# Reordered splits, stores and roundings at eleven places of a GLA + latent-attention inference step

## The reference

```
gla_mixer:  q, k, v, r = h @ w_q, h @ w_k, h @ w_v, h @ w_r
            lg = log_sigmoid((h @ w_gk1) @ w_gk2 + b_gk) / 16
            b = cumsum(lg) within a chunk of 64;  k*exp(-b), q*exp(b), k*exp(b_last-b)
            o, S = recurrence over the chunks;  out = (rmsnorm(o) * silu(r)) @ w_o
mla_mixer:  cq = rmsnorm(h @ w_dq);  q = cq @ w_uq;  q_rope = rope(q[..., 128:])
            q_abs = q_nope @ w_uk;  scores over 4096 cached rows (paged) + new rows
            out = softmax(scores) @ ckv @ w_uv @ w_o
conv_ffn:   u = h @ w_gate;  c = conv_b + causal taps of width 3 over u
            out = (gelu(c) * (h @ w_up)) @ w_down
trunk:      layer 0: x += norm(gla(norm x));  x += norm(conv_ffn(norm x))
            layer 1: x += norm(mla(norm x));  x += norm(conv_ffn(norm x))
```

## Time and profile before

| what | value |
|---|---|
| median of 3 runs | 1475.28 us (1474.13 to 1475.62) |
| the profiled execution's own time | 1475.53 us |
| its span on the core | 1473.8 us |
| TensorE, VectorE, ScalarE, GpSimd busy | 97%, 62%, 46%, 38% |
| mean granted TensorE clock | 0.995 |
| moved by DMA | 160.19 MB, 109 GB/s |

### The profile page before, as it was taken

How to read it: one execution, slowest core, us unless ns; L and a number is a source line. 1 busy time by engine, 2 the same in 40 slices (tenths; PEclk the granted TensorE clock), 3 DMA queues, 4 the chain that set the end, 5 groups by cost and what they waited for, 6 DMA issues and landing times. The chain is left out here.

```text
span 1473.8 us, 31036 instructions
## 1 busy us (share of the span) xinstructions
PE 1428.7 (97%) x11156; PEld 1304.1 (88%) x11156; DVE 916.4 (62%) x1506; ACT 676.6 (46%) x1281; POOL 561.1 (38%) x552
## 2 busy tenths in 40 slices
PE   6999999999999999999999999999999999999997
PEld 6999998988999999998986566666989999999997
DVE  4742446499999993236466744433579999995223
ACT  5433345375666672216313444443265565665211
POOL 1333111235555554341330044441315555554433
PEclk9999999999999999999999999999999999999999
DMA  4242322213232323222321099981212323223231
GB/s 165 72 144 86 115 86 101 91 58 104 97 103 96 103 88 112 97 79 96 104 81 33 4 283 287 280 261 46 102 47 87 115 85 114 85 84 109 82 98 66
DMA packets 56714, 160.19 MB, mean 109 GB/s; under 512 B 7633, under 2 KB 27602, under 8 KB 55330
## 3 DMA queue, kind: packets, MB, share of 16 engines
q1 hardware_dynamic: 50466, 137.82, 28.1%
q0 software_dynamic: 6144, 20.98, 4.6%
HBM read 150.72 MB, written 8.05 MB: 108 GB/s over the span
## 5 line engine op out<-in xcount | busy, mean ns | idle before, releaser
L716 POOL TENSOR_TENSOR w_l<-w_raw,w_h 128x1408 fp32r<-128x1408 f32 (+1 forms) x50 | 143.8, 2878 | 274.8 <-ACT w_h L837 153.3
L711 POOL TENSOR_TENSOR w_l<-w_raw,w_h 128x1024 fp32r<-128x1024 f32 (+2 forms) x42 | 108.1, 2575 | 284.1 <-ACT w_h L837 274.3
L2272 PE MATMUL lin<-xg_h,w_h 128*128 128x272 f32 x848 | 195.4, 303 | 17.1 <-DVE xg_l L1449 10.6
L2272 PE MATMUL lin<-xg_l,w_h 128*128 128x272 f32 x848 | 184.7, 290 | 0.0
L2272 PE MATMUL lin<-xg_h,w_l 128*128 128x272 f32 x848 | 184.6, 290 | 0.0
L2625 PE MATMUL lin<-xq_h,wq_r 128*128 128x272 f32 x864 | 170.1, 289 | 3.7 <-DVE xq_l L1835 3.6
L2625 PE MATMUL lin<-xq_h,w_h 128*128 128x272 f32 x576 | 166.3, 289 | 2.4 <-DVE xq_l L1835 2.3
L2625 PE MATMUL lin<-xq_h,w_l 128*128 128x272 f32 x576 | 166.0, 288 | 0.0
L2625 PE MATMUL lin<-xq_l,w_h 128*128 128x272 f32 x576 | 165.4, 287 | 0.0
L2272 PEld LDWEIGHTS lin<-xg_h,w_h 128*128 128x128 f32 x848 | 138.2, 191 | 25.0 <-issue 13.5
L837 ACT ACTIVATE w_h<-w_raw 128x1024 fp32r<-128x1024 f32 (+2 forms) x71 | 77.2, 1088 | 171.1 <-PE lin L2272 139.1
(11 more groups left out here) (407 smaller groups left out, 3238.4 us busy)
## 6 DMA issues: line engine op xcount, KB each, us to landing
wq_raw<-w SPq DMA_DIRECT2D x38, 1024.0 KB, 5.0
w_raw<-w SPq DMA_DIRECT2D x61, 512.0 KB, 3.5
w_raw<-w SPq DMA_DIRECT2D x30, 704.0 KB, 4.1
pages<-cache SPq DMA_DIRECT2D x128, 160.0 KB, 3.8
pages<-cache POOLq DMA_DIRECT2D x128, 160.0 KB, 3.8
St<-state SPq DMA_DIRECT2D x4, 1024.0 KB, 6.0
gla_s<-St SPq DMA_DIRECT2D x4, 1024.0 KB, 3.9
w_raw<-w SPq DMA_DIRECT2D x4, 576.0 KB, 3.8
```

Source lines behind the costliest of these rows:

```text
L711: g.tensor_tensor(w_l[:, p % 2, 0:n], raw_panel(p)[:, 0:n], w_h[:, p % 2, 0:n].bitcast(F32), ALU.subtract).then_inc(w_lo, 1)
L716: g.tensor_tensor(w_l[:, p % 2, 0:n], w_raw[:, p % 2, 0:n], w_h[:, p % 2, 0:n].bitcast(F32), ALU.subtract).then_inc(w_lo, 1)
L2272: last = mm(lin[:, 2 * out_set + half, 0:HALF], w[:, slot, (w0 + k) * P:(w0 + k + 1) * P], (v[ch] if isinstance(v, list) else v[:, ch, :]) ...
```

## The change

Nothing is computed differently; instructions of one engine change places, and a few waits move with them. The places, in order of the program: (A) ACT splits panel 1 after chunk 5 of x, not chunk 3, and TensorE sums the squares two steps later. (B) DVE makes the running sums of the gates of head 0 one step sooner. (C) SP loads panel `P_G2 + 3` ahead of the last state's store; ACT waits for the store's landing behind the split of panel `P_G2 + 2`, still ahead of the squares; DVE updates the last sample state ahead of `gated_lo(5)`, two groups of instructions sooner. (D) In the third direct product, the second tile's chunk 6 is multiplied after the first tile's last chunk. (E) In both layers, ACT and DVE make the first pair's quarters ahead of some work on plain channel 3. (F) Of the keys of each two heads, the first are copied out between the two products of a rotation. (G) At the end of the prompt's attention the order of the last `probs` and of the last heads' rounding changes. (H) `score_unit` takes its three waits one by one, each before the matmuls that need it. (I) At the last unit of pages ACT splits `P_M3` before `page_probs`, and TensorE's first half of that panel is cut in chunks 4, 2 and 2 instead of 5, 2 and 1.

```diff
--- before.py
+++ after.py
@@ -591,10 +591,11 @@
     load_panel(P_G2 + 2, io["w8"][P_G2 + 2])
+    load_panel(P_G2 + 3, io["w8"][P_G2 + 3])
     state_out(3)
...
     sp_.dma_start(io["gla_p"], S[:]).then_inc(gla_out, 16)
-    load_run(io["w8"], P_G2 + 3, P_G2 + 3, P_F0A - P_G2 - 4)
+    load_run(io["w8"], P_G2 + 4, P_G2 + 4, P_F0A - P_G2 - 5)
     for k in range(3):
@@ -945,7 +946,7 @@
             square(i, x[:, i, :])
-        if chs[0] == 2:
+        if chs[0] == 4:
             split_hi(1)
@@ -1064,11 +1065,12 @@
             split_hi(p0 + m + 2)
+            if n == 1 and m == 0:
+                act.wait_ge(st_out[0], 32)
             act.wait_ge(evac, t0 + m + 1)
...
-    act.wait_ge(st_out[0], 32)
     output_squares(P_G2, T_G2, 1, ("ffn_pre", 0))
@@ -1199,10 +1201,11 @@
         quarter_hi(None, 0, 0)
+        quarter_hi(None, 0, 1)
         plain_tap(3)
-        quarter_hi(None, 0, 1)
         quarter_hi(None, 0, 2)
         quarter_hi(None, 0, 3)
+        quarter_hi(None, 0, 4)
@@ -1222,13 +1225,12 @@
         part(None, 0, 0)
-        quarter_hi(None, 0, 4)
         quarter_hi(None, 0, 5)
         part(None, 0, 1)
-        plain_gelu(3)
         input_hi(5)
...
         quarter_hi(None, 0, 6)
+        plain_gelu(3)
         input_hi(6)
@@ -1344,12 +1346,18 @@
     probs(0)
-    for n in range(NM):
-        if n + 1 < NM:
-            probs(n + 1)
+    for n in range(NM - TILES):
+        probs(n + 1)
         if n % TILES == 1 and n > TILES:
...
         probs_turned(n)
+    probs(NM - 3)
+    probs(NM - 2)
+    probs_turned(NM - 4)
+    probs(NM - 1)
+    for n in range(NM - 3, NM):
+        probs_turned(n)
+    head_hi(H_M - 2)
     head_hi(H_M - 1)
@@ -1393,9 +1401,10 @@
         pages_turned(4 * unit_ + 3)
+    act.wait_ge(qk_ps, UNITS)
+    split_hi(P_M3)
     page_probs(UNITS - 1)
     page_probs_turned(UNITS - 1)
-    split_hi(P_M3)
     split_hi(P_M3 + 1)
@@ -1546,8 +1555,8 @@
             gate((t - 1) // 2)
-        if t in (2, 4, 6, 8):
-            gate_sums((t - 2) // 2)
+        if t in (1, 4, 6, 8):
+            gate_sums((t - 1) // 2)
@@ -1636,11 +1645,11 @@
     gated_lo(4)
+    sample_states(H_G - 1, NSEQ // 2 - 1)
     gated_lo(5)
...
     gated_lo(DC - 1)
-    sample_states(H_G - 1, NSEQ // 2 - 1)
@@ -1940,10 +1949,9 @@
         sum_lo(None, 0, 2)
-        plain_conv(3)
-        input_lo(3)
         last_sum(None, 0)
         sum_lo(None, 0, 4)
+        input_lo(3)
@@ -1960,8 +1968,9 @@
         input_lo(4)
+        plain_conv(3)
+        input_lo(5)
         plain_product(3)
-        input_lo(5)
         sum_lo(None, 0, 6)
@@ -2027,12 +2036,19 @@
+    def keys_out(h):
+
+        complete(T_UK + h)
+        v.tensor_copy(kn[:, h, :], lin[:, 2 * ((T_UK + h) % 2), :]).then_inc(evac, 1)
+
     def rotate(n, dst):
...
         v.tensor_tensor(halves(rot[:, 0, :]), px[:, 2:4, 0:HALF], halves(sin[:]), ALU.mult).then_inc(rot_done, 1)
+        if n:
+            keys_out(2 * n - 2)
         v.tensor_tensor(rot[:, 1, :], dst, cos[:], ALU.mult).then_inc(rot_done, 1)
@@ -2076,9 +2092,7 @@
         rotate(1 + n, q[:, 8 + n, :])
-        for h in (2 * n, 2 * n + 1):
-            complete(T_UK + h)
-            v.tensor_copy(kn[:, h, :], lin[:, 2 * ((T_UK + h) % 2), :]).then_inc(evac, 1)
+        keys_out(2 * n + 1)
     for k in range(2):
@@ -2130,8 +2144,9 @@
             maxima(n + 2)
-        if n % TILES == 2 and n > TILES:
+        if n % TILES == 2 and TILES < n < NM - TILES:
             head_lo(n // TILES - 1)
+    head_lo(H_M - 2)
     head_lo(H_M - 1)
@@ -2363,8 +2378,9 @@
                 pair_squares(n + 1, k)
-            for m in range(DIRECT):
-                last = direct_chunk(t + m, w[:, m, :], x_, k, (1,) if k < AHEAD[n] else (0, 1))
+            for m in range(DIRECT - 1 if n == 3 and k == DC - 2 else DIRECT):
+                for j in range(k - 1, k + 1) if n == 3 and m and k == DC - 1 else (k,):
+                    last = direct_chunk(t + m, w[:, m, :], x_, j, (1,) if j < AHEAD[n] else (0, 1))
                 if k == DC - 1:
@@ -2383,7 +2399,7 @@
                     last.then_inc(w_used, 1)
-            if k == DC + 3:
+            if k == DC + 5:
                 stat(n)
@@ -2876,13 +2892,12 @@
         b = u // 2
-        pe.wait_ge(ta_done, 4 * u + 4)
-        pe.wait_ge(tv_done, 4 * u + 4)
-        pe.wait_ge(tr_done, 2 * u + 2)
-        for r in range(KC):
+        for r, sem_ in ((0, ta_done), (1, tv_done)):
+            pe.wait_ge(sem_, 4 * u + 4)
             for j in range(4):
...
                    tile_position=(0, 32 * j))
+        pe.wait_ge(tr_done, 2 * u + 2)
         for j in range(4):
@@ -2955,13 +2970,13 @@
     take_panel(P_M3)
-    first_half(P_M3, T_M3, range(0, 5))
+    first_half(P_M3, T_M3, range(0, 4))
     pe.wait_ge(fin_v, 2)
     nc.tensor.transpose(banks[1][:, 0:NSEQ], flt[:, 1, :], ident[0:NSEQ, 0:NSEQ]).then_inc(fin_ps, 1)
-    first_half(P_M3, T_M3, range(5, 7))
+    first_half(P_M3, T_M3, range(4, 6))
     pe.wait_ge(fin_v, 5)
     mm(banks[3][:, 0:NSEQ], gsum[:], fl[:, 0, :], start=True, stop=True).then_inc(fin_ps, 1)
-    first_half(P_M3, T_M3, range(7, DC))
+    first_half(P_M3, T_M3, range(6, DC))
```

## The result

The changed kernel takes 1462.78 us (median of 4 runs, 1462.42 to 1463.12), the kernel before, run beside it, 1474.71 us (median of 4, 1474.13 to 1475.62). The ratio is 0.9922, with a 95% interval of 0.991 to 0.9934: faster by 0.8%, about 12 us. The profiled execution of the changed kernel took 1462.42 us, 13.1 less than that of before (1475.53). Forecast were 1462.3 and, between the profiled executions, 12.95.

What follows compares the result with a forecast made beforehand. TensorE, busy for 97% of 1473.8 us, was taken to set the end. Terms summing to 12.95 us came off the profiled 1475.53, giving 1462.6, less 0.25: 1462.3; range 1458.0 to 1467.5, some 0.85 of the chance.

Steps and rivals of the forecast that it cites:

- the first pairs: First pair of both layers: TensorE's waits for `xq_l` shrink, 1.4 us a layer, 2.8 in all; ends 0 and 5.9.
- the clock: Half-clock stretches behind the waits at the gates and state store go with those waits, 1.7 us each.
- the keys: Key copies: TensorE's wait for `kn` behind `rot` goes, gain 1.0 us; ends 0.5 and 1.2.
- the attention's end: Waits of 1.43 and 0.78 us go but return at group 7's pages; gain 0.1, counted as 0; ends 0 and 2.2.
- the start: Panel 1: the 0.49 us wait for the squares' sum goes, the 1.32 comes back; gain 0.5, ends 0 and 1.8.
- the last unit: Waits for `kr_t` (0.78), POOL's `w_l` (0.69) and `selw` (0.48) go; gain 1.95 us, ends 0 and 1.95.
- Gates and state store: Waits of TensorE: 0.8 us goes at the gates; 2.5 of 3.11 goes at the state store, 0.6 stays.
- the step that said a dip goes with its wait: At the gates, half clock only follows a wait in these rows, so it goes too: 0.8 + 1.7 = 2.5 us.
- the forecast's two terms: First pair, DVE's time: idle 0.86 us goes, plus about half of one 1.1 stall beside POOL, 0.5; per layer.
- the second rival: First pairs gain nothing because DVE's stalls beside POOL follow it: 2.8 us lost, 1465.1; chance 0.12.
- the pages are the limit: Attention's end: page issues cap the gain; the rival that they don't would add 2.2 us, 1460.1, chance 0.10.
- the slower case: Loop of pairs: one more 1.1 us DVE stall per pair makes TensorE wait 0.92 in each, 1491.7; chance 0.04.

Runs made afterwards that it cites:

- old_load_order: Changed kernel with panel `P_G2 + 3` again loaded behind the last state's store, ACT's wait staying where the change put it; 1463.16 us.
- no_gates: Changed kernel with the running sums of the gates one copy later again, as before the change; 1464.98 us.

## Why the prediction was right

The time, 1462.3 against 1462.78, and most of its parts were right, because the argument took one wait after the other and asked each time what else was late behind it. That the sum came within 0.2 us between the profiled executions is partly luck: the first pairs were 0.7 too high and the clock 0.4, the keys 0.5 too low, the attention's end 0.3, the start and the last unit 0.2 each, and these cancel. The undone parts cost 3.9 (C), 2.2 (B), 2.0 (E), 0.8 (G, H), 1.2 (F), 1.1 (I) and 0.0 (D). With 0.7 for A, which was only read from the traces and not undone, that is 11.9, and the two medians stand 11.9 apart. The agreement is closer than the numbers allow: the kernel before has medians from 1473.8 to 1475.3 in the four sets of runs, as the three kinds of run fall in them, and A is known to about 0.4. What can be said is that nothing over about 1 us is left unexplained.

- *Start.* As forecast: the wait of 1.32 is one of 1.38 at 16.76, behind an `xg_l` of 2.37 us beside POOL's `w_l`, and the 0.49 is gone.
- *Gates and state store.* The waits were right to 0.1. The clock was right as a mechanism; the step that said a dip goes with its wait took the dip at 42.5 as certain to be there. It is there in some executions, so the median gains less than the profiled execution: 11.9 against 13.1. The waits that stay (0.72, 0.79, 1.11, 1.38) have no dip behind them in the changed kernel's trace. Its four runs lie within 0.7 us, where those of before spread over 1.5.
- *State store, the reason.* The forecast put the gain down to the split's moved wait and had the store issued no later than before. DVE's earlier update issues it sooner (236.93, where the old place would give about 239.7, 242.91 less the 3.2 us that the kernel is ahead). By the traces that update alone would do in the old order of the loads, and so would ACT's moved wait alone, since the next split has time to spare; neither was run by itself. The third load ahead of the store does nothing for the time (`old_load_order`).
- *First pairs.* Mis-sized: 2.1 in place of 2.8. The last product of the first pair starts 1.5 us sooner, against 1.4 forecast, but not by the forecast's two terms. DVE's idle time goes from 0.86 to 0.27, so 0.6 and not 0.86 is gained there; its stalls beside POOL were three before (a `c` of 1.74 where its like takes 0.80, `xq_l` of 2.38 and 2.20) and are two now (1.84 and 2.27), 0.9 less and not 0.5. So the stalls did follow POOL in part, as the second rival had it. The step that failed is that everything behind would keep the gain: 0.5 is lost again in the second pair, where TensorE waits 0.29 for ACT's `part`, which it hadn't waited for. And product 5 waits for `a`, not for its `xq_l`.
- *Keys.* Mis-sized: 1.2 by the undone kernel and 1.5 by the traces, against the 1.0 of the one wait. The next wait of the same kind, 0.24 at 772.86 in the trace before, went too.
- *Attention's end.* Right in its size and its cause. The place was wrong: the first group to be late is group 3, at 847, not group 7, since only group 7's row had been set beside its landing.
- *Last unit.* Right to 0.2; the small DVE instructions beside POOL's `w_l` at 1003.86 take 0.15 and 0.27 us, so no stall shows.
- *The rivals.* The dips did not come back; the pages are the limit; the store no longer holds the split; a pair of the loop takes 10.53 us with DVE busy for 10.35, so the slower case had nothing behind it.

## What to carry to other kernels

Where one engine is busy for 97%, take the gain of a reordering wait by wait, and for each write down what arrives next and how much later; the waits whose successor was 0.1 us behind were worth nothing until that successor was moved too. An edit that shows no gain may be half of one: look for the limit that took its place before it is dropped. Compare the starts of the same instruction in both traces: that tells a gain kept from one that is given back a few microseconds later.

## What the runs showed of the hardware

A wait of 0.80 us at the gates is followed by a stretch at 1.2 GHz in the trace of the kernel before (clock 0.62) and by none in that of `no_gates` (1.00), and the times of `no_gates` are of two kinds (1463.4 to 1463.6 and 1465.0 to 1465.4 us). So one profile can't say whether a short wait costs itself or itself and 1.6 us. Waits of 0.72 to 1.38 us elsewhere had none behind them in the trace of the changed kernel.

Two instructions that DVE and POOL run side by side can hold each other up: the same `xq_l` takes 1.28 us alone and 2.27 beside POOL's `w_l`, and with POOL moved away the delay falls on the next DVE instruction that POOL meets (1.80 against 0.74).

Issuing a page whose number is already in a register takes 0.6 us on POOL's queue against 1.15 with the read in front of it (six in 3.54 us), and both queues together then moved 357 GB/s where the busy share of the DMA engines had already read 0.90 at 286. A high share there was no proof that the transfers were the limit.
